# Five modulation parts summed by TensorE with the weights stationary, VectorE's other parts spread thinner over both v sweeps

## The chip, the cores and the metric

The kernel runs on one core of one Trainium2 chip. Five engines work in it, each through its own instruction stream: TensorE (PE; its weight loads are shown apart as PEld), VectorE (DVE), ScalarE (ACT), GpSimd (POOL) and SyncE (SP), which issues most of the transfers from HBM. TensorE's clock has two levels, 1.2 and 2.4 GHz; the profile shows the granted level as 0.50 and 1.00. The metric is the device time of one execution in microseconds.

## What is computed

A two-layer trunk over 128 context tokens and 256 latent tokens with 1024 channels. Layer 0 has windowed attention with pooling channels, layer 1 a convolution module; each is followed by PEER, a retrieval among 16,384 experts. Ahead of each of these four steps stands a normalisation that is modulated by a conditioning vector (`c_ctx` for the context tokens, `c` for the latent ones), and each step's result is gated by it:

```python
def adaln(cvec, w, b):
    m = jax.nn.silu(cvec) @ w + b
    return jnp.split(m[:, None, :], 6, axis=-1)

    mp = adaln(c_ctx[None, :], mod_w[l], mod_b[l])      # per layer l; ms likewise with c
    hp = modulate(rms_norm(xp, norm_mix_g[l]), mp[0], mp[1])     # h * (1 + scale) + shift
    ...                                                          # attention or convolution
    xp = xp + mp[2] * op
    hp = modulate(rms_norm(xp, norm_ffn_g[l]), mp[3], mp[4])
    xp = xp + mp[5] * peer(hp, ...)                     # xs likewise with ms

def conformer_conv(h, w1, b1, w_dw, b_dw, ln_g, ln_b, w2, b2):
    a = h @ w1 + b1
    a = a[..., :CONV_DIM] * jax.nn.sigmoid(a[..., CONV_DIM:])
    a = depthwise_conv(a, w_dw, width=31) + b_dw
    a = jax.nn.silu(layer_norm(a, ln_g, ln_b))
    return a @ w2 + b2
```

So there are twelve modulation parts, six per layer (shift, scale, gate, twice); each is the product of two vectors with a 1024x1024 matrix in fp32, and `mod_w` holds 48 MB in all.

## The kernel before

The activations are kept transposed, 128 channels on the partitions, eight chunks (`KC`) of channels, 384 tokens. Projections run through 512 KB weight blocks: SP loads a block into the ring `raw` (four slots, `load`, `stream`), ScalarE makes its rounded half `w_hi` (L691), GpSimd the rest `w_lo` (L599), and TensorE multiplies three times (L1511 to L1513, L1528 to L1530). A program of this kind has no scheduler: each engine runs the order in which the code is written, and semaphores tie the engines together.

In order of time there are: the head with the first norm; the projection `in` with ten blocks; attention (before it VectorE's rope, L1153 to L1155, then TensorE's scores, L1561; nine `in` blocks stand ahead of the first scores); `out`; the norm, the query projection and the choice of experts; the sweep over 128 u blocks; the **first v sweep** (L1745, 760.0 to 1304.4 us); the convolution with its norm, `w1` (16 blocks), the depthwise taps (TensorE at L1652 for some channel chunks, VectorE at L1247 for the others, spread over w1 and after it), mean and variance (L1663, L1667) and `w2` (eight blocks); and then queries, u sweep and **second v sweep** (2053.2 to 2516.2 us) of layer 1. In a v sweep SP loads the v blocks, VectorE weighs gathered rows and assembles the operand (L1432), ScalarE loads stored activations and applies the weights (L936 and on).

A modulation part is eight blocks of 512 KB, its matrix transposed: an output channel per partition. Part 0 (the first shift) is different before: TensorE keeps the two conditioning columns `cvec` stationary and passes its rows through in 512 columns (`first_shift`, L1772), ScalarE copies the two rows of sums, and TensorE turns them into columns (L1777). The other 88 blocks are summed by VectorE: `mod_group` (L1047) multiplies a block, 128x1024, by one of the two conditioning vectors that all partitions hold (`c_all`, in the tile `keys`, 1 MB, which ScalarE's `conditioning` passes through Silu), and sums along the row; two groups per block, and every four blocks `mod_bias` (L1053). The blocks come through a ring of four slots, `mod_w` in `hots` or later `mod_late` in `work`; SP loads a block when the group four blocks earlier is summed (`mod_load`). Eight blocks (part 1, the scale) are summed in the head, twelve in a loop ahead of the rope, twelve during attention and `out`, and 56 in the first v sweep, four per eight v blocks; for these SP loads c again at the start of that sweep, since the PEER keys have taken its place, and ScalarE waits for it there. The loads of `in` blocks 4 to 9 stand in SP's queue between pairs of modulation loads.

Of the kernel before, what the change touches and what calls it, by code (L numbers as in the profile page):

```python
# [38 lines left out]
P = 128  # L39
# [78 lines left out]
SUM_BLOCKS = MOD_BLOCKS - KC  # L118
MSLOTS = 4
MOD_EARLY = 4 * KC  # L120
MOD_FIRST = KC
LATE_MODS = MOD_EARLY - 12
MOD_ROUNDS = (SUM_BLOCKS - MOD_EARLY) // MSLOTS
# [61 lines left out]
def build(nc, io):  # L185
    ctx = ExitStack()
    with ctx:
# [71 lines left out]
        a_out = ga[:, :, :].rearrange("p a t -> p (a t)")[:, 0:4 * ND].rearrange("p (a t) -> p a t", a=4)  # L259
        unread = ga[:, :, :].rearrange("p a t -> p (a t)")[:, 0:D].bitcast(BF16).rearrange("p (g d) -> p g d", g=2)  # L260
# [42 lines left out]
        shift_rows = work[0:2, sums_at + 5 * D:sums_at + 6 * D]  # L303
        assert qk_at + 3 * D <= v_at and sums_at + 6 * D <= place[0]
# [5 lines left out]
        odd = region(2, CONV_OUT)  # L310
        tap_sum = (ps[:, 6, 0:CONV_OUT], ps[:, 7, 0:CONV_OUT])
# [36 lines left out]
        shift_summed = sem("shift_summed")  # L348
        shift_copied = sem("shift_copied")
        shift_done = sem("shift_done")  # L350
# [98 lines left out]
        def _(sp):  # L449
# [26 lines left out]

            def gates(i, span, n):
# [5 lines left out]
            def mod_load_late(k):  # L483

                sp.dma_start(mod_late[:, k, :], one(io["mod_w"], MOD_EARLY + k)).then_inc(mod_raw[k], 16)
# [15 lines left out]
            n = MOD_FIRST  # L501
# [5 lines left out]
            for m in range(RING):  # L507
                if n < MOD_EARLY - 8:
                    mod_load(n)
                    n += 1  # L510
                stream("out", m, 1, 1)
# [7 lines left out]
            for layer in range(DEPTH):  # L519
# [20 lines left out]
                if layer == 0:  # L540
                    sp.wait_ge(s_done, HS)
                    conditioning()
                    for k in range(MSLOTS):
                        mod_load_late(k)

                def turn(i, final, mods):

                    for j in range(TURN):
# [10 lines left out]
                        if j // 8 in mods and j % 2:  # L559
                            sp.wait_ge(mod_summed, i * TURN + (2 * MOD_EARLY - 8 + j + 1))  # L560
                            k = j % 8 // 2
                            sp.dma_start(mod_late[:, k, :],
                                         one(io["mod_w"], i * (TURN // 8 * MSLOTS) + (MOD_EARLY + j // 8 * MSLOTS + k))
                                         ).then_inc(mod_raw[k], 16)

                if layer == 0:

                    turn(0, False, range(1, 4))
                    with sp.Fori(1, TURNS - 1) as i:
                        turn(i, False, range(4))  # L570
                    turn(TURNS - 1, True, range(MOD_ROUNDS - 4 * (TURNS - 1)))
                else:
                    with sp.Fori(0, TURNS - 1) as i:
                        turn(i, False, ())
                    turn(TURNS - 1, True, ())
                if layer == 0:
                    sp.wait_ge(mod_summed, 2 * SUM_BLOCKS)
# [98 lines left out]
        def _(act):  # L676
# [31 lines left out]
            nc.scalar.activation(cvec[:, :, :], cvec[:, :, :], ACT.Silu).then_inc(c_ready, 1)  # L708
            conditioning(1)
# [36 lines left out]
            def gated(name, layer, part):  # L746

                m0 = M0[name]
                act.wait_ge(mod_ready, [MOD_EARLY - 2 * KC, SUM_BLOCKS][layer] // MSLOTS)
# [175 lines left out]
            def experts(layer):  # L925
# [48 lines left out]
                if layer == 0:  # L974
                    conditioning(2)
# [40 lines left out]
        def _(dve):  # L1016
# [23 lines left out]
            def mod_group(i, step, block, k, g, ring=mod_w):  # L1040
# [9 lines left out]
            def mod_bias(i, step, block):  # L1050
                dve.wait_ge(mod_summed, i * (2 * step) + (2 * (block + MSLOTS)))
                at = bass.ds(i * step + (block + KC), MSLOTS)
                tt(mod[:, at, :], sums[:, :, :], broad(mod_b[:, at], [P, MSLOTS, 2], 2), ALU.add).then_inc(mod_ready, 1)  # L1053

            def mod_four(i):
                for k in range(MSLOTS):
                    for g in range(2):
                        mod_group(i, MSLOTS, 0, k, g)
# [36 lines left out]
            def normalise(n):  # L1095
# [7 lines left out]
                if n == 0:  # L1103

                    dve.wait_ge(c_ready, 2)
                    rounds(dve, MOD_FIRST // MSLOTS, mod_four, peel=True)
                    dve.wait_ge(mod_ready, MOD_FIRST // MSLOTS)
                    mod_scales([0])
                    dve.wait_ge(shift_done, 1)
# [750 lines left out]
```

## Time and profile before

| | us |
|---|---|
| median of 3 runs | 2535.1 (2529.44 to 2536.3) |
| profiled execution | 2537.79 |
| its span | 2536.0 |
| head, up to the first product of `in` | 0 to 47.1 |
| `in`, and wait for the rope | 47.1 to 114.3 |
| attention, `out` | 114.3 to 235 |
| norm, queries, choice of experts | 235 to 404 |
| u sweep, layer 0 | 404 to 760.0 |
| first v sweep | 760.0 to 1304.4 |
| convolution, with its norm | 1304.4 to 1510 |
| norm, queries, choice of experts | 1510 to 1703 |
| u sweep, layer 1 | 1703 to 2053.2 |
| second v sweep | 2053.2 to 2516.2 |

TensorE is busy 91% of the span, VectorE 69%, GpSimd 44%, ScalarE 36%. In a row of the timeline the first number is the start, the second the time until the end of the last of the merged instructions, and brackets tell how long the engine had been idle and what released it. A row by stretch gives each engine's busy time, TensorE's granted clock, the share of the 16 DMA engines' time and what they moved.

### The profile page before, as it was taken

How to read it: one execution, taken by the hardware profiler on the slowest of the kernel's cores; microseconds unless marked ns; L12 is line 12 of the kernel's file. 1: busy time of each engine (PE TensorE's matmuls, PEld its weight loads, DVE VectorE, ACT ScalarE, POOL GpSimd, SP SyncE). 2: the span in 40 equal slices, each digit the busy share in tenths (PEclk: the TensorE clock that was granted, in tenths of full speed). 3: DMA queues.
4: the chain of work that ended last, by engine and by line, in shares of the span. 5: the costliest groups of instructions: out<-in, count | busy, mean ns of one | idle time of the engine just before them, and what ended most of it. 6: DMA issues, size and time to landing. Idle time of an engine off the chain costs nothing.

```text
span 2536.0 us, 38385 instructions
## 1 busy us (share of the span) xinstructions
PE 2296.9 (91%) x11829; PEld 1702.4 (67%) x11829; DVE 1752.9 (69%) x3945; ACT 911.0 (36%) x1694; POOL 1110.3 (44%) x612
## 2 busy tenths in 40 slices
PE   6797999999998888888989779999999989999998
PEld 3676999999983333333359469989999854444443
DVE  7986798878435766677768955898886345545555
ACT  3253445666541111111034354556666520000002
POOL 2613487777872222222215034677777841111110
PEclk8798999999999999899899889999999999999999
DMA  7423368999999999999954022588999999999995
GB/s 300 158 77 125 109 225 289 371 380 392 380 401 399 389 397 404 391 393 400 377 202 133 0 67 100 167 270 329 383 387 386 391 394 397 402 407 405 400 402 188
DMA packets 195783, 771.19 MB, mean 304 GB/s; under 512 B 21728, under 2 KB 22880, under 8 KB 160224
## 3 DMA queue, kind: packets, MB, share of 16 engines
q1 hardware_dynamic: 120512, 402.81, 42.8%
q0 software_dynamic: 36864, 268.45, 26.7%
q10 hardware_dynamic: 38304, 98.71, 10.0%
q8 instruction: 45, 0.74, 0.1%
q14 instruction: 58, 0.48, 0.1%
HBM read 701.08 MB, written 68.81 MB: 304 GB/s over the span
## 4 chain that ended last, share of the span: by engine, by line
PE 50%; DMA 18%; issue 13%; DVE 11%; POOL 6%; ACT 1%; ACTq 0%; SPq 0%; DVEq 0%; POOLq 0%
PE ps L1745 23%; DMA raw<-in_v 11%; PE ps L1511 7%; PE ps L1512 7%; PE ps L1513 7%; POOL w_lo L599 5%; DMA raw<-in_u 4%; PE ps L1727 4%; DVE ga L1047 1%; DVE ps L1328 1%; DVE work L1330 1%; DMA w_hi<-g_dram 1%; PE ps L1680 1%; ACT w_hi L691 1%; DVE work L1305 1%
## 5 line engine op out<-in xcount | busy, mean ns | idle before, releaser
L599 POOL TENSOR_TENSOR w_lo<-raw,w_hi 128x1024 fp32r<-128x1024 f32 x330 | 799.5, 2432 | 594.5 <-ACT w_hi L691 593.6
L1745 PE MATMUL ps<-raw,work 128*128 128x512 f32 x2048 | 913.4, 607 | 95.1 <-DMA raw<-in_v 82.5
L1745 PEld LDWEIGHTS ps<-raw,work 128*128 128x128 f32 x2048 | 393.9, 194 | 613.4 <-issue 572.7
L1511 PE MATMUL ps<-h_hi,w_hi 128*128 128x256 f32 (+1 forms) x2560 | 776.0, 303 | 26.3 <-POOL w_lo L599 26.2
L1512 PE MATMUL ps<-h_lo,w_hi 128*128 128x256 f32 (+1 forms) x2560 | 757.6, 296 | 0.0
L1513 PE MATMUL ps<-h_hi,w_lo 128*128 128x256 f32 (+1 forms) x2560 | 757.1, 296 | 0.0
L1511 PEld LDWEIGHTS ps<-h_hi,w_hi 128*128 128x128 f32 x2560 | 495.0, 193 | 35.0 <-POOL w_lo L599 32.6
L1512 PEld LDWEIGHTS ps<-h_lo,w_hi 128*128 128x128 f32 x2560 | 495.4, 194 | 0.0
L1513 PEld LDWEIGHTS ps<-h_hi,w_lo 128*128 128x128 f32 x2560 | 494.6, 193 | 0.0
L691 ACT ACTIVATE w_hi<-raw 128x1024 fp32r<-128x1024 f32 x330 | 347.6, 1056 | 130.0 <-DMA raw<-in_u 54.1
L936 ACT ACTIVATE wgt<-dots (+1 forms) x256 | 53.1, 208 | 755.3 <-DVE uv_stat L1389 218.3
L617 POOL DMA_INDIRECT work<-in_uv,picked x64 | 73.1, 1142 | 245.9 <-DVE ps L1381 236.8
L617 POOL DMA_INDIRECT hots<-in_uv,picked x64 | 73.8, 1153 | 242.2 <-DVE ps L1381 231.1
L1432 DVE TENSOR_TENSOR work<-work,w_hi 128x256 f32<-128x256 f32 x128 | 53.8, 424 | 175.4 <-PE ps L1745 130.1
L1408 DVE TENSOR_SCALAR hots<-ps,work 128x128 f32<-128x128 f32 x512 | 173.6, 400 | 0.0
L956 ACT ACTIVATE work<-ps 128x512 f32<-128x512 f32 x128 | 145.5, 1137 | 66.0 <-PE ps L1727 62.2
L1432 DVE TENSOR_TENSOR work<-work 128x256 f32<-128x256 f32 x128 | 53.6, 423 | 161.8 <-PE ps L1745 120.3
L919 ACT ACTIVATE ga<-ps 128x256 f32<-128x256 f32 x256 | 97.6, 381 | 176.9 <-PE ps L1513 172.4
L1047 DVE CUSTOM_DVE_ANT_0 ga<-work,keys 128x1024 bf16<-128x1024 f32 x112 | 136.3, 1217 | 20.7 <-issue 11.0
L1404 DVE TENSOR_TENSOR hots<-ps,work 128x512 f32<-128x512 f32 x128 | 87.8, 686 | 82.3 <-PE ps L1727 82.2
L617 POOL DMA_INDIRECT hf<-in_uv,picked x64 | 71.7, 1121 | 155.2 <-DVE ps L1381 151.4
L1727 PE MATMUL ps<-hots 128*128 128x128 f32 x1024 | 135.3, 275 | 1.6 <-ACT work L956 1.6
(196 smaller groups left out, 2416.2 us busy)
## 6 DMA issues: line engine op xcount, KB each, us to landing
raw<-in_u SPq DMA_DIRECT2D x256, 512.0 KB, 6.1
raw<-in_v SPq DMA_DIRECT2D x256, 512.0 KB, 8.8
a_dram<-ga ACTq DMA_DIRECT2D x128, 256.0 KB
g_dram<-work ACTq DMA_DIRECT2D x16, 2048.0 KB, 12.3
work<-a_dram ACTq DMA_DIRECT2D x120, 256.0 KB, 8.0
work<-in_mod_w SPq DMA_DIRECT2D x56, 512.0 KB, 13.0
hots<-in_mod_w SPq DMA_DIRECT2D x32, 512.0 KB, 3.6
raw<-in_wq SPq DMA_DIRECT2D x32, 512.0 KB, 3.5
```

The lines of the kernel that those rows point to most:

```text
L599: nc.gpsimd.tensor_tensor(w_lo[:, m % RING, :], raw[:, m % RING, :], w_hi[:, m % RING, :].bitcast(F32), ALU.subtract).then_inc(lo_ready, 1)
L617: nc.gpsimd.indirect_dma_start(out=uv_rows[q % UVBUFS], out_offset=None, in_=io[f"uv{layer}"], in_offset=bass.IndirectOffsetOnAxis(ap=pick ...
L691: nc.scalar.activation(w_hi[:, m % RING, :], raw[:, m % RING, :], ACT.Copy).then_inc(hi_ready, 1)
L956: nc.scalar.activation(stage[:, s, :, tok:tok + TOK].rearrange("p k t -> p t k"), ps[:, ACC, :].rearrange("p (t k) -> p t k", k=N_KEYS), A ...
L1047: nc.vector.tensor_tensor_reduce(unread[:, g, :], ring[:, k, :], c_all[:, g, :], 1.0, 0.0, ALU.mult, ALU.add, accum_out=sums[:, k, g:g + 1 ...
L1408: last = ts(oh1[:, b, q, :], iota_p, col_key[:, 0, tok], col_g[:, tok], ALU.is_equal, ALU.mult)
L1432: tt(wf[:, j % WBUFS, :].rearrange("p (c t) -> p c t", t=CHUNK), a_in[:, j % (2 * A_PAIRS), :].rearrange("p (c t) -> p c t", t=CHUNK), g_i ...
L1511: mm(out, w_hi[:, s, cols], h_hi[:, k, first:], start=n == 0, stop=False)
L1512: mm(out, w_hi[:, s, cols], h_lo[:, k, first:], start=False, stop=False)
L1513: last = mm(out, w_lo[:, s, cols], h_hi[:, k, first:], start=False, stop=n == KC - 1)
L1727: last = mm(ps[:, ACC, q * P:(q + 1) * P], oh2[:, b, q, :], oh1[:, b, q, :], start=True, stop=True)
L1745: last = mm(ps[:, Y_DENSE[NT - ND_TILES + t] + half, :], wf[:, b, t * P:(t + 1) * P], raw[:, s, half * 512:(half + 1) * 512], start=first, ...
```

## The change

Parts 0, 1, 8, 9 and 10 (layer 0's first shift and scale; layer 1's gate of the convolution and its second shift and scale) are now made by TensorE with the weights stationary: a chunk of 512 KB, 128 input channels by 1024 output channels, is eight stationary 128x128 tiles, and the two conditioning columns of `cvec` are passed through each (`part_sums`). The result lies with the channels on the partitions, in PSUM, and needs no turning. 16 chunks stand in the head behind the first column sums (`first_parts`), 24 in the convolution: five ahead of w1, one after each of w1's blocks 6 to 12, six between the taps on TensorE and the mean, six ahead of w2. They come through their own ring of five slots, `part_w`, loaded by SP between the blocks of w1 and w2.

VectorE sums the seven other parts, 56 blocks: twelve in the loop, now its first and with the group for the context vector reading c from PSUM (`c_ps`, written by ScalarE), twelve in attention and `out` as before, 24 in the first v sweep (one per four v blocks), eight in the second. c is loaded a third time, at the second sweep's start. In the head SP issues c's load behind the 16 chunks.

```diff
+PE_PARTS = (0, 1, 8, 9, 10)
+SUM_PARTS = (2, 3, 4, 5, 6, 7, 11)
+PSLOTS = 5
+CHUNKS_NORM, CHUNKS_W1, CHUNKS_MEAN, CHUNKS_W2 = range(0, 5), range(5, 12), range(12, 18), range(18, 24)
-MOD_EARLY = 4 * KC
-MOD_FIRST = KC
+MOD_EARLY = 3 * KC
+MOD_FROM = (MOD_EARLY, 6 * KC)
+MOD_ROUNDS = (3 * KC // MSLOTS, KC // MSLOTS)
...
+        c_ps = ps[:, 6:8, :].rearrange("p a b -> p (a b)")
...
+            for n in range(KC):
+                if n % 4 == 3:
+                    load("in", n // 4, n // 4)
+                head_chunk(n)
+            for n in range(KC, HEAD_CHUNKS):
+                head_chunk(n)
             conditioning()
-            for k in range(KC):
-                if k % 4 == 3:
-                    load("in", k // 4, k // 4)
-                sp.dma_start(shift_w[k], one(io["shift_w"], k)).then_inc(shift_loaded[k], 16)
-                mod_load(k)
+            for n in range(MSLOTS):
+                mod_load(n)
...
-            n = MOD_FIRST
+            n = MSLOTS
             for m in range(RING, 10):
                 for _ in range(2):
                     mod_load(n)
                     n += 1
                 stream("in", m, 1, 1)
...
-                if layer == 0:
-                    sp.wait_ge(s_done, HS)
-                    conditioning()
-                    for k in range(MSLOTS):
-                        mod_load_late(k)
+                sp.wait_ge(s_done, (layer + 1) * HS)
+                conditioning()
+                for k in range(MSLOTS):
+                    mod_load_late(layer, k)
...
-                        if j // 8 in mods and j % 2:
+                        if span in mods and j % 4 == 3:
...
-                    stream("w1", RING, 16 - RING, 4)
-                    stream("w2", 0, 8, 4)
+                    sp.wait_ge(rows_used, SLOTS)
+                    for n in CHUNKS_NORM:
+                        part_chunk(n)
+                    stream("w1", RING, 2, 2)
+                    for n in range(5, 10):
+                        part_chunk(n)
+                        stream("w1", n + 1, 1, 1)
+                    ...
...
             nc.scalar.activation(cvec[:, :, :], cvec[:, :, :], ACT.Silu).then_inc(c_ready, 1)
+            act.wait_ge(c_loaded, 16)
+            nc.scalar.activation(c_ps, c_all[:, 0, :], ACT.Silu).then_inc(c_ready, 1)
+            act.wait_ge(c_ready, 2)
             conditioning(1)
...
-                    act.wait_ge(shift_summed, 1)
-                    nc.scalar.activation(shift_rows, ps[0:2, ACC + 2:ACC + 4, :].rearrange("p a b -> p (a b)"),
-                                         ACT.Copy).then_inc(shift_copied, 1)
...
-                if layer == 0:
-                    conditioning(2)
+                conditioning(2 + layer)
...
-                nc.vector.tensor_tensor_reduce(unread[:, g, :], ring[:, k, :], c_all[:, g, :], 1.0, 0.0,
+                nc.vector.tensor_tensor_reduce(unread[:, g, :], ring[:, k, :],
+                                               c_all[:, g, :] if g or first is None else first, 1.0, 0.0,
                                                ALU.mult, ALU.add, accum_out=sums[:, k, g:g + 1]).then_inc(mod_summed, 1)
...
-                    dve.wait_ge(c_ready, 2)
-                    rounds(dve, MOD_FIRST // MSLOTS, mod_four, peel=True)
-                    dve.wait_ge(mod_ready, MOD_FIRST // MSLOTS)
+                    dve.wait_ge(part_done, HEAD_CHUNKS)
+                    settle(tt(mod[:, 0:2 * KC, :], ps[:, ACC + 1, 0:4 * KC].rearrange("p (a b) -> p a b", b=2),
+                              broad(mod_b[:, 0:2 * KC], [P, 2 * KC, 2], 2), ALU.add))
                     mod_scales([0])
...
             def convolution():
-                blocks("w1")
+                part_chunks(CHUNKS_NORM)
+                blocks("w1", beside=CHUNKS_W1)
...
+                pe.wait_ge(conv_taken, KC - CONV_DVE)
+                part_chunks(CHUNKS_MEAN)
...
+                part_chunks(CHUNKS_W2)
                 blocks("w2")
...
-            def first_shift():
...
+            def part_sums(w, bank, col, k):
+
+                for o in range(KC):
+                    last = mm(ps[:, bank, col + 2 * o:col + 2 * o + 2], w[:, o * P:(o + 1) * P], cvec[:, k, :],
+                              start=k == 0 and o == 0, stop=k == KC - 1 and o == KC - 1)
+                last.then_inc(part_done, 1)
```

The change moves instructions in three places that matter below. First, SP's queue in the head. `in_c` is c, `in_shift_w` part 0, `in_mod_w` VectorE's blocks and `in_part_w` TensorE's chunks. Before (the last two rows then go on in turn, eight of each):

```order
L489 DMA ident<-in_c_ident 128x128
L489 DMA cvec<-in_c_cols 128x16
L452 DMA keys<-in_c 128x2048
L494 DMA work<-in_shift_w 128x1024
L457 DMA hots<-in_mod_w 128x1024
```

After:

```order
L505 DMA cvec<-in_c_cols 128x16
L486 DMA work<-in_part_w 128x1024 x3
L467 DMA raw<-in_in 128x1024
L486 DMA work<-in_part_w 128x1024 x4
L467 DMA raw<-in_in 128x1024
L486 DMA work<-in_part_w 128x1024 x9
L458 DMA keys<-in_c 128x2048
L463 DMA hots<-in_mod_w 128x1024 x4
L467 DMA raw<-in_in 128x1024 x2
```

c stood ahead of everything but the small tables, and stands behind 16 chunks and two `in` blocks now; only four of VectorE's blocks are loaded ahead of its loop, where eight were.

Second, SP's queue in the first v sweep, between its first v blocks, before:

```order
L461 DMA raw<-in_v 128x1024 x2
L562 DMA work<-in_mod_w 128x1024
L461 DMA raw<-in_v 128x1024
L480 DMA w_hi<-g_dram 128x2x512
L461 DMA raw<-in_v 128x1024
L562 DMA work<-in_mod_w 128x1024
L461 DMA raw<-in_v 128x1024 x2
```

The same part of the sweep after:

```order
L467 DMA raw<-in_v 128x1024 x7
L496 DMA work<-g_dram 128x2x512
L467 DMA raw<-in_v 128x1024 x2
L576 DMA work<-in_mod_w 128x1024
L467 DMA raw<-in_v 128x1024
L496 DMA work<-g_dram 128x2x512
L467 DMA raw<-in_v 128x1024 x3
L496 DMA work<-g_dram 128x2x512
L576 DMA work<-in_mod_w 128x1024
```

Between two modulation loads there were two v blocks, and there are four.

Third, TensorE at the end of the convolution, from w1's last products over the taps, mean and variance to w2. Before:

```order
L1513 MATMUL ps<-h_hi,w_lo 128x384
L1544 REGISTER_ALU
L1544 COMPARE_AND_BRANCH
L1652 MATMUL ps<-work,hots 128x399 x62
L1663 MATMUL ps<-work,ones 128x399 x8
L1667 MATMUL ps<-work,ones 128x399 x8
L1528 MATMUL ps<-h_hi,w_hi 128x384
```

After:

```order
L1551 MATMUL ps<-h_hi,w_lo 128x384
L1699 MATMUL ps<-work,hots 128x399 x62
L1817 MATMUL ps<-cvec,work 128x2 x48
L1710 MATMUL ps<-work,ones 128x399 x8
L1714 MATMUL ps<-work,ones 128x399 x8
L1817 MATMUL ps<-cvec,work 128x2 x48
L1566 MATMUL ps<-h_hi,w_hi 128x384
```

Two groups of 48 products with two columns each, six chunks, stand ahead of the mean's and of w2's products; the wait for the taps' results on VectorE now comes behind the first of them.

## Rows read from the trace of the kernel before

**Rows 1.** By stretch: first v sweep, second v sweep (first line: the columns)

```profile
core 0: us, PE busy (x) PEld busy (x) DVE busy (x) ACT busy (x) POOL busy (x), PEclk, DMA share, GB/s
760.00:1304.40 544.40, 467.73 (x1025) 200.43 (x1026) 369.02 (x610) 63.82 (x181) 118.80 (x77) 0.94 0.98 386
2053.20:2516.20 463.00, 445.60 (x1026) 193.91 (x1027) 241.34 (x368) 41.35 (x165) 73.43 (x77) 1.00 0.98 385
```

**Rows 2.** TensorE's waits for v blocks, first and second sweep (us, times, longest)

```profile
PE ps L1745 <- DMA raw<-in_v: 67.1, 23, 8.1
...
PE ps L1745 <- DMA raw<-in_v: 15.4, 11, 3.6
```

**Rows 3.** DMA issues: the first sweep's modulation blocks (count, KB, us to landing)

```profile
work<-in_mod_w SPq DMA_DIRECT2D x56, 512.0 KB, 13.0
```

**Rows 4.** Timeline (start, us): TensorE, then ScalarE, early in the first sweep

```profile
779.51 20.85 PE L1745 MATMUL ps<-raw,work 128*128 128x512 f32 x43 [9.02 <-DVE work L1432]
...
773.87 1.91 ACT L703 ACTIVATE keys<-keys 128x2048 f32<-128x2048 f32 x1 [11.77 <-DMA keys<-in_c]
```

**Rows 5.** Weight loads (ns min/median/max), ranges and clock by stretch, passes at 37.76

```profile
40.70:42.70 2.00, 1.94 (x16) 1.86 (x16) 2.00 (x5) 0.00 (x0) 0.00 (x0) 1.00 1.14 356
43.20:47.10 3.90, 0.00 (x0) 0.00 (x0) 3.30 (x12) 1.49 (x4) 0.00 (x0) 0.50 1.03 393
...
1703.20:1704.90 1.70, 1.64 (x8) 1.64 (x9) 0.06 (x2) 0.31 (x1) 1.31 (x1) 0.50 1.01 424
...
L1777 PEld LDWEIGHTS ps<-ident,work x16: 181/187/187, 40.7 to 42.4; 2*128 2x128 f32 x16
...
L1772 PEld LDWEIGHTS ps<-work,cvec x32: 80/85/127, 16.0 to 38.6; 128*2 128x2 f32 x32
...
L1716 PEld LDWEIGHTS ps<-ident,work x12: 179/230/231, 406.6 to 1704.2; 128*128 128x128 f32 x12
...
1703.26 1.14 PEld L1716 LDWEIGHTS ps<-ident,work 128*128 128x128 f32 x6 [4.45 <-DVE gate_s L1371]
...
37.76 1.88 PE L1772 MATMUL ps<-work,cvec 128*2 128x512 f32 x4 [1.93 <-DMA work<-in_shift_w]
```

**Rows 6.** Timeline: column sums, first products, first scores (TensorE); first scaling (VectorE)

```profile
8.91 7.15 PE L1551 MATMUL ps<-hf,ones 128*128 128x384 f32 x16 [8.91 <-DVE hf L1139]
...
47.14 0.66 PE L1528 MATMUL ps<-h_hi,w_hi 128*128 128x384 f32 x1 [4.46 <-DVE h_lo L1127]
...
114.26 0.79 PE L1561 MATMUL ps<-work 64*128 64x128 f32 x2 [15.15 <-DVE work L1155]
...
44.63 1.41 DVE L1118 SCALAR_TENSOR_TENSOR hf<-x,scales,uv_stat 128x128 f32<-128x128 f32 x4 [0.32 <-DVE mod L1110]
```

**Rows 7.** Loop before attention, in block 8, taps (timeline; L1247 by line)

```profile
55.77 1.22 DVE L1047 CUSTOM_DVE_ANT_0 ga<-hots,keys 128x1024 bf16<-128x1024 f32 x1
...
56.91 3.37 DVE L1047 CUSTOM_DVE_ANT_0 ga<-hots,keys 128x1024 bf16<-128x1024 f32 x1
...
109.14 1.48 DVE L1153 TENSOR_TENSOR work<-ps,work 128x1280 f32<-128x1280 f32 x1
...
83.53 0.43 SPq L461 DMA_DIRECT2D raw<-in_in  x1
...
L1247 DVE SCALAR_TENSOR_TENSOR ps<-work,dw,ps x168: 626/631/635, 1334.1 to 1448.6; 128x399 f32<-128x399 f32 x168
```

**Rows 8.** Convolution: w1 by stretch, then timeline of TensorE and VectorE

```profile
1320.70:1390.50 69.80, 69.54 (x384) 69.27 (x385) 60.75 (x126) 28.12 (x45) 37.80 (x16) 0.96 0.36 113
...
1320.72 0.66 PE L1528 MATMUL ps<-h_hi,w_hi 128*128 128x384 f32 x1 [8.33 <-DVE h_lo L1127]
...
1449.90 1.70 PE L1663 MATMUL ps<-work,ones 128*128 128x399 f32 x2 [12.64 <-DVE work L1251]
...
1468.25 0.66 PE L1528 MATMUL ps<-h_hi,w_hi 128*128 128x384 f32 x1 [7.78 <-DVE h_lo L1136]
...
1349.22 0.74 DVE L1226 SCALAR_TENSOR_TENSOR work<-ps,b,work 128x128 f32<-128x128 f32 x2 [1.08 <-PE ps L1513]
```

More of the change, by code:

```diff
@@ L302, in build @@
                    for n in range(count)]
-        shift_rows = work[0:2, sums_at + 5 * D:sums_at + 6 * D]
-        assert qk_at + 3 * D <= v_at and sums_at + 6 * D <= place[0]
+        assert qk_at + 3 * D <= v_at and sums_at + 5 * D <= place[0]
         a_pad = region(KC, CONV_IN, at=0)
@@ L347, in build @@
         shift_loaded = [sem(f"shift_loaded{k}") for k in range(KC)]
-        shift_summed = sem("shift_summed")
-        shift_copied = sem("shift_copied")
-        shift_done = sem("shift_done")
+        part_loaded = [sem(f"part_loaded{k}") for k in range(PSLOTS)]
+        part_done = sem("part_done")
+        parts_taken = sem("parts_taken")
         mod_summed = sem("mod_summed")
@@ L506, in _ @@
                 stream("in", m, 1, 1)
[L507 to L511, printed above, removed]
+            stream("out", 0, RING, RING)
             while n < MOD_EARLY - 4:
@@ L576, in _ @@
[L576 to L580 removed]
+                assert MOD_ROUNDS == (2 * (TURNS - 1), 2)
+                turn(0, False, (1,))
+                with sp.Fori(1, TURNS - 1) as i:
+                    turn(i, False, () if layer else (0, 1))
+                turn(TURNS - 1, True, ())
@@ new lines, in _ @@
+                if layer == 0:
+                    sp.wait_ge(mod_summed, 2 * MOD_FROM[1])
+                    sp.dma_start(keys[:, :, :], io["keys"][1]).then_inc(keys_loaded, 16)
+                    sp.wait_ge(rows_used, SLOTS)
[5 more added lines that the diff above has]
+                        stream("w1", n + 1, 1, 1)
+                    for n in range(10, 15):
+                        stream("w1", n + 1, 1, 1)
+                        part_chunk(n)
+                    for n in range(15, 17):
+                        part_chunk(n)
+                    stream("w2", 0, RING, RING)
+                    for n in range(17, 22):
+                        part_chunk(n)
+                    stream("w2", RING, 2, 2)
+                    for n in range(22, 24):
+                        part_chunk(n)
+                    stream("w2", RING + 2, 2, 2)
@@ L1036, in _, with mod_group @@
             dve.wait_ge(first_loaded, 5 * 16)
-            def mod_group(i, step, block, k, g, ring=mod_w):
+            def mod_group(i, step, block, k, g, ring=mod_w, first=None):
                 if k == 0 and g == 0:
@@ L1057, in mod_four @@
                     for g in range(2):
-                        mod_group(i, MSLOTS, 0, k, g)
+                        mod_group(i, MSLOTS, 0, k, g, first=c_ps)
                 mod_bias(i, MSLOTS, 0)
@@ L1259, in convolution @@
                 taps(len(pending))
+                dve.wait_ge(part_done, HEAD_CHUNKS + KC)
+                at = slice((6 + 2) * KC, (6 + 3) * KC)
+                settle(tt(mod[:, at, :], ps[:, ACC + 1, 0:2 * KC].rearrange("p (a b) -> p a b", b=2),
+                          broad(mod_b[:, at], [P, KC, 2], 2), ALU.add))
+                tt(gb2[:, :, :], mod[:, at, :], broad(cvecs[:, 3, :], [P, KC, 2], 2), ALU.mult).then_inc(parts_taken, 1)
                 dve.wait_ge(mean_done, 1)
@@ L1271, in convolution @@
                 pipelined(scaled, low_operand)
+                dve.wait_ge(part_done, HEAD_CHUNKS + 3 * KC)
+                for at, src in ((6 + 3, ps[:, ACC, CONV_OUT + 1:CONV_OUT + 1 + 2 * KC]), (6 + 4, ps[:, ACC + 2, 0:2 * KC])):
+                    cols = slice(at * KC, (at + 1) * KC)
+                    last = tt(mod[:, cols, :], src.rearrange("p (a b) -> p a b", b=2), broad(mod_b[:, cols], [P, KC, 2], 2),
+                              ALU.add)
+                    last.then_inc(parts_taken, 1)
+                dve.wait_ge(parts_taken, 3)
+                mod_scales([3])
                 for k in range(KC):
@@ L1532, in project_pair, with blocks @@
                             last.then_inc(block_done, 1)
-            def blocks(name, chunks=()):
+            def blocks(name, chunks=(), beside=()):
                 m, r = M0[name], R0[name]
@@ L1543, in blocks @@
                     project(0, 4, m + j, r + j)
+                if beside:
+                    for j in range(4, dict(SEGMENTS)[name]):
+                        project(0, 4, m + j, r + j)
+                        if j - 6 in range(len(beside)):
+                            part_chunks(beside[j - 6:j - 5])
+                    return
                 with pe.Fori(1, dict(SEGMENTS)[name] // 4) as i:
```

113 lines of the change are left out of this document (55 added, 58 removed).

## The prediction

> **What bounds the kernel now.** I read the busy time by stretch first. The two sweeps over the 128 v blocks do the same work twice, but the first lasts 544.4 us and the second 463.0, both with the DMA engines 98% busy at 386 and 385 GB/s [rows 1]. TensorE's waits say the same: on v blocks 67.1 us in the first sweep, 15.4 in the second [rows 2]. What the first has and the second has not is 56 modulation blocks of 512 KB [rows 3] and the 1 MB of c: 58 units of 512 KB for 81.4 us, 1.40 us each; by bandwidth a unit is 524,288 B / 386 GB/s = 1.36 us. So the first sweep is bound by bytes. Elsewhere other things end last: in the head VectorE's sums of eight modulation blocks, behind which the first projection starts at 47.14; before attention VectorE's loop over twelve more blocks, behind which TensorE waits 15.15 us [rows 6, 7]; in the convolution first TensorE's w1, then VectorE's chain of taps, for whose end TensorE waits until 1449.90 [rows 8].
>
> The sum is made against the profiled execution, 2537.8 us (span 2536.0), 2.7 above the median 2535.1.
>
> **1. First sweep.** 32 of its 56 modulation blocks go: 32 x 1.36 = 43.5 us less (by 1.40 it would be 44.8). The floor does not get in the way: TensorE is busy 467.7 us there and VectorE 369.0 [rows 1], and VectorE loses 64 sums. I take **-43.5** (-40 to -45). The stop at its start stays: TensorE idles 9.02 us because ScalarE sat 11.77 us waiting for c [rows 4].
>
> **2. Second sweep.** It gains 8 blocks and c, 10 units, at 98% DMA: **+13.6**. ScalarE now waits for c here too, with everything it would store, load and weight behind it. In the first sweep that stop didn't stop the transfers, so it is within the unit price; the upper bound adds its 9.0 us: +22. Below, +10: TensorE's other waits could absorb some.
>
> **3. Price of a chunk.** A part is now eight chunks of eight fp32 products 128x128 by 128x2, each in two passes, so a chunk is 16 pairs of weight load and 2-column matmul. The nearest rows are the 16 pairs of the transposes at L1777, at full clock: their weight loads lie within 1.86 us, the last takes 0.187, so they start (1.86 - 0.187) / 15 = 0.112 us apart [rows 5]. A chunk is then 16 x 0.112 = **1.79 us**. The clock will not stay up: it stood at 0.50 (1.2 GHz) shortly after those pairs [rows 5]. A load of 128 columns took 187 ns at 2.4 GHz and 230 at 1.2 (L1716, where the clock was 0.50), one of 2 columns 85 and at its slowest 127 [rows 5]: the difference, the columns' part, is 102 and 103 ns at either clock, and the 43 ns that are added are overhead that pairs overlap. So I keep 1.79. The upper bound by rows is the pairs of L1716 with their slow loads, (1.14 - 0.23) / 5 = 0.18 us apart, but with 128 moving columns behind each [rows 5]: 2.9 us a chunk. Below, a pair cannot be cheaper than the columns' 102 ns: 1.63.
>
> Here two rules of one page can be weighed. The Trainium skill ("TensorE: Matmul & The Clock Gate", "LDWEIGHTS (loading the stationary operand)") prices a load by its columns alone, columns / 1.2 ns, 107 ns here, an estimate of 1.71 us a chunk; the 112 ns agree. Its "Part 1: The HAM clock gate (the "warmup" mystery)" has the gate pass only half the pulses to the array, and were the loads to go by that clock, this change would lose, as in rival A; the equal 102 and 103 ns speak against it.
>
> **4. Head.** Removed: 16 of VectorE's sums, the 512-column passes, ScalarE's copy and the transposes. Added on TensorE behind the column sums, which end at 16.06 [rows 6]: 16 chunks x 1.79 = 28.6, ending at 44.7, where VectorE's scaling began at 44.63 before [rows 6]: 0. Chunks arrive faster than they are used (17 units of 1.36 us are 23 us, and they start before the column sums end). But c now comes behind 16 chunks, and ScalarE's wait for it stands ahead of its root and first two w_hi. GpSimd's two passes for w_lo then fall beside VectorE's scaling, where each can cost a VectorE operation with two SBUF inputs about 2.15 us (3.37 - 1.22, [rows 7]): +4.5 (3 to 6).
>
> **5. Loop and attention.** The 24 sums of the loop run from 55.77 to 109.14, 53.4 us for 24 x 1.22 = 29.3 of work; the rest is collisions with GpSimd and three short biases [rows 7]. After the change every other sum reads c from PSUM. An operation with one PSUM input never lost anything: 626 to 635 ns over 168 taps, beside GpSimd's passes [rows 7]. Halving the 24 us of loss makes the loop some 12 us shorter; since a GpSimd pass that spares one sum often meets the next, I take -9. Against that, the loads of `in` move back in SP's queue: block 8, the last that stands before the first scores, was issued at 83.53 once six of the loop's twelve blocks were summed, and 15.6 us later, at 114.26 - 15.15 = 99.11, TensorE was through with it [rows 6, 7]; now it waits for ten of twelve. The loop starts at 60.3 and takes 53.4 - 9 = 44.4; the rope behind it, 5.1 us from VectorE's start at 109.14 to the first scores at 114.26 [rows 6, 7], ends at 109.8. Ten of twelve blocks are done at 60.3 + 37 = 97.3, and 97.3 + 15.6 = 112.9: block 8 comes last now. So 1.4 us are won; the 15.6 hold a block at low clock, which a busier TensorE may run faster, and I take **-2** for head and attention together (-9 if block 8 is quick and the loop loses less, +6 if the loop loses as often as before).
>
> **6. Convolution.** Ahead of w1 TensorE idles 8.33 us for the norm [rows 8]; five chunks take 8.95: +0.6. In w1, seven chunks after blocks 6 to 12. TensorE bounds this stretch (69.5 of 69.8 us) and VectorE's serial taps wait for it, 1.08 us per pair of blocks [rows 8], so 7 x 1.79 = 12.5 delay both: +12.5. Should the clock fall in each of these gaps, part of the next block (69.5 / 16 = 4.35 us) runs at half speed, some 2 us each time: +14 more. Against it, after a wait of 1.93 us the four passes at 37.76 still took 1.88 us, full speed [rows 5]; I take 0. Before the mean, six chunks (10.7) in the 12.64 us in which TensorE waits for the last taps: 0. That cover is thin; gone, it costs up to 10.7. Ahead of w2, six chunks (10.7) where it idled 7.78: +2.9. Sum **+16** (11 if VectorE catches up in w1, 30 if the clock falls in each gap). Chunks' loads are hidden: DMA is 36% busy there [rows 8]. The few VectorE operations on 16 columns that turn sums into mod, gb2 and scales lie in waits for TensorE: 0; without that cover, under 1 us.
>
> **Sum:** -43.5 + 13.6 - 2 + 16 = -15.9. From 2537.8 that is 2521.9, and against the median 2535.1 - 15.9 = **2519**. The terms' bounds, not all at once, give 2506 to 2538.
>
> **The rivals.**
> A, slower: weight loads go by the lower clock. A pair then takes 2 x 0.112 us and a chunk 3.6. The head's chunks end at about 68 (the first three at full clock: 16.06 + 3 x 1.79 + 13 x 3.6), +23, of which the shorter loop takes back 6.5 (the 4.5 of the head and the 2 above); the convolution pays 5 x 3.6 - 8.3 = 9.7, 12.5 in w1 (full clock there), 21.6 - 12.6 = 9, and 21.6 - 7.8 = 13.8, together 45. Sum: -29.9 + 16.5 + 45 = +31.6: 2567. Between 1.79 us (-15.9) and 3.6 (+31.6) the sign turns at a chunk of 2.4 us, 150 ns a pair. For it: the clock does fall. Against: the 102 and 103 ns.
> B: the wait for c at the second sweep's start idles TensorE on top of the bytes: +9, 2528. For it: TensorE is busy 445.6 of 463 us there, with little room to recover. Against: DMA stayed at 98%.
> C, the change doesn't bring its bytes' worth: part of the 81.4 us is the stop at the start and the clock (0.94 against 1.00), not bytes, and the first sweep gives only half, 22. Then -22 + 13.6 - 2 + 16 = +5.6: 2541. Against: the waits for v, 52 us apart.
>
> **How the numbers follow.** Forecast 0.66, A 0.12, B 0.12, C 0.10. A measurement of this kernel can tell about 0.3%, 7.6 us: faster is below 2527.5, slower above 2542.7. Of the forecast 0.57 is faster and 0.09 the same; of B 0.06 and 0.06; of C 0.02 faster, 0.06 the same, 0.02 slower; A is slower. Faster 0.65, same 0.21, slower 0.14. The range leaves out most of A and a little below: 2500 to 2547.
>
> **What would show it.** First sweep about 501 us, its waits for v near 25; second about 477. Pairs of the chunks 0.11 us apart, also at clock 0.50; first projection at about 51, first scores near 112. The last tap some 13 us later relative to w1's start, no wait of VectorE's for the mean's chunks, and w2's start 16 us later relative to the norm. It is wrong if a chunk takes over 2.4 us, if the first sweep stays above 515, or if the second passes 490.

## The result, and the profile after

The changed kernel is slower: 2544.42 us (median of 20 runs, 2538.89 to 2550.64) against 2529.11 (20 runs), a ratio of 1.0059, 95% interval 1.0049 to 1.0068, some 15 us. 2519 was forecast, 16 us faster than the median known then. The time lies in the stated range, but on the other side, on rival A's. The profiled executions are 2544.5 and 2537.8 us; the latter is 8.7 above its kernel's own median, which matters for the first sweep (see e5_cps).

The stages, from TensorE's first and last products in each (us):

| stage | before | after | change | forecast |
|---|---|---|---|---|
| start to the first product of `in` | 47.1 | 70.9 | +23.7 | +4.5 |
| to the first scores | 67.1 | 52.1 | -15.0 | -6.5 |
| attention to the end of the u sweep | 645.7 | 646.7 | +1.0 | 0 |
| first v sweep | 544.6 | 496.3 | -48.3 | -43.5 |
| norm ahead of w1, chunks | 16.2 | 20.8 | +4.6 | +0.6 |
| w1, chunks | 69.8 | 81.9 | +12.1 | +12.5 |
| taps and mean, chunks | 69.9 | 74.4 | +4.5 | 0 |
| to w2, chunks | 7.8 | 15.1 | +7.3 | +2.9 |
| w2 to the end of the u sweep | 585.0 | 584.2 | -0.8 | 0 |
| second v sweep | 462.9 | 480.4 | +17.5 | +13.6 |

Both sweeps did what was forecast. Busy time by stretch, columns as in [rows 1], first sweep, second sweep and w1:

```profile
769.73:1265.84 496.11, 460.40 (x1024) 196.46 (x1025) 298.67 (x472) 63.82 (x181) 95.57 (x77) 0.97 0.99 390
2042.50:2522.70 480.20, 450.83 (x1024) 195.01 (x1025) 259.60 (x402) 63.80 (x181) 80.61 (x77) 0.98 0.97 382
1286.83:1368.70 81.87, 81.63 (x497) 81.34 (x498) 56.19 (x112) 25.71 (x39) 37.83 (x16) 0.97 0.46 161
```

TensorE's waits for v blocks, first and second sweep, which answer to [rows 2]:

```profile
PE ps L1793 <- DMA raw<-in_v: 26.0, 20, 5.7
...
PE ps L1793 <- DMA raw<-in_v: 19.5, 13, 6.0
```

The DMA engines are as busy as before, and the waits went from 67.1 to 26.0 us in the first sweep.

The loss is in the chunks. TensorE's timeline in the head, then the clock in two stretches of it and over all chunks, and its weight loads by line (L1817 is `part_sums`):

```profile
17.30 50.52 PE L1817 MATMUL ps<-cvec,work 128*128 128x2 f32 x256
70.88 0.66 PE L1566 MATMUL ps<-h_hi,w_hi 128*128 128x384 f32 x1 [3.06 <-DVE h_lo L1153]
...
19.30:21.30 2.00, 2.00 (x20) 2.00 (x19) 0.00 (x0) 0.00 (x0) 0.00 (x0) 1.00 0.57 162
25.30:35.30 10.00, 10.00 (x49) 10.00 (x48) 0.00 (x0) 0.00 (x0) 0.00 (x0) 0.50 0.50 158
17.30:67.82 50.52, 50.52 (x257) 50.43 (x255) 4.28 (x4) 8.54 (x9) 5.00 (x2) 0.54 0.62 226
...
L1817 PEld LDWEIGHTS ps<-cvec,work x640: 186/333/338, 17.0 to 1458.0; 128*128 128x128 f32 x160
```

The 16 chunks were to take 28.6 us and take 50.5. At clock 1.00, 20 pairs (a weight load and its 2-column product) go through in 2.0 us; at 0.50, 49 in 10.0, 0.205 us a pair and 3.3 us a chunk. By the records TensorE never stops in these 50 us (its weight loads fill 50.43 of 50.52), and the clock falls all the same. The convolution shows the same (TensorE's timeline: ahead of w1, one chunk between w1's blocks, ahead of the mean, mean, ahead of w2):

```profile
1273.71 13.26 PE L1817 MATMUL ps<-cvec,work 128*128 128x2 f32 x80
...
1318.74 1.84 PE L1817 MATMUL ps<-cvec,work 128*128 128x2 f32 x16
...
1411.15 17.69 PE L1817 MATMUL ps<-cvec,work 128*128 128x2 f32 x96 [0.68 <-ACT work L894]
1428.70 6.99 PE L1710 MATMUL ps<-work,ones 128*128 128x399 f32 x16
...
1443.01 15.42 PE L1817 MATMUL ps<-cvec,work 128*128 128x2 f32 x96
1458.30 0.67 PE L1566 MATMUL ps<-h_hi,w_hi 128*128 128x384 f32 x1
```

A chunk alone between two blocks of w1 takes 1.84 us, as forecast; five in a row take 13.26 instead of 8.95, six take 17.69 and 15.42 instead of 10.7. The mean's wait for VectorE [rows 8] is gone: the mean's 16 products now start right behind the chunks.

The loop ahead of attention was better than forecast (VectorE's first two sums, and the rope behind the last), and c came later (ScalarE's first Silu):

```profile
79.51 1.21 DVE L1075 CUSTOM_DVE_ANT_0 ga<-hots,ps 128x1024 bf16<-128x1024 f32 x1
...
80.65 2.67 DVE L1075 CUSTOM_DVE_ANT_0 ga<-hots,keys 128x1024 bf16<-128x1024 f32 x1
...
116.12 1.49 DVE L1179 TENSOR_TENSOR work<-ps,work 128x1280 f32<-128x1280 f32 x1
...
46.66 1.03 ACT L736 ACTIVATE ps<-keys 128x1024 f32<-128x1024 f32 x1 [34.96 <-DMA keys<-in_c]
```

The loop takes 36.6 us where it took 53.4 [rows 7]; the sums with c in PSUM all take 1.21 to 1.22.

### The profile page after: what moved, and what is told of

It is laid out like the page before. It is cut to its first block, busy times and chain, and to the rows that moved or that the text cites. A ratio compares the mean times of both kernels' runs of the same rounds, so it can differ in the third digit from the quotient of the medians.

```text
span 2542.7 us, 38958 instructions
## 1 busy us (share of the span) xinstructions
PE 2375.3 (93%) x12421; PEld 1793.9 (71%) x12421; DVE 1670.6 (66%) x3812; ACT 933.1 (37%) x1711; POOL 1087.3 (43%) x612
## 4 chain that ended last, share of the span: by engine, by line
PE 54%; DMA 15%; issue 13%; DVE 10%; POOL 5%; ACT 1%; SPq 0%; ACTq 0%; DVEq 0%; POOLq 0%
PE ps L1793 24%; DMA raw<-in_v 10%; PE ps L1549 7%; PE ps L1550 7%; PE ps L1551 7%; POOL w_lo L625 5%; PE ps L1775 4%; DMA raw<-in_u 4%; PE ps L1817 2%; DVE ps L1367 1%; DVE work L1369 1%; PE ps L1728 1%; DMA a_dram<-ga 1%; DVE ga L1075 1%; ACT w_hi L717 1%
## 5 line engine op out<-in xcount | busy, mean ns | idle before, releaser
L643 POOL DMA_INDIRECT uv_stat<-in_uv,picked x64 | 66.6, 1041 | 152.8 <-DVE ps L1420 149.2
```

What stands on the lines that cost most here:

```text
L643: nc.gpsimd.indirect_dma_start(out=uv_rows[q % UVBUFS], out_offset=None, in_=io[f"uv{layer}"], in_offset=bass.IndirectOffsetOnAxis(ap=pick ...
```

## The experiments

The theory after this reading: it is the granted clock that doubles the weight loads, and the clock falls because the products pass only two columns each. The rivals: many loads in a row are slow for another reason, and the clock only goes along with it; the sweeps lose by their stops; the chunks in w1 or the head's loss are made up elsewhere. "Kernel before" in the ratios is run beside each on the same chip.

**e1_hold: a wide product ahead of each chunk of the head.**

```diff
                     pe.wait_ge(shift_loaded[n % KC], 16 * (n // KC + 1))
+                    mm(ps[:, PROJ, :], ones[:, :], shift_w[n % KC][:, 0:512], start=True, stop=True)
                     part_sums(shift_w[n % KC], ACC + 1, n // KC * 2 * KC, n % KC)
```

> The changed kernel, with one fp32 product of 512 moving columns (two passes, 0.86 us at full clock, into an unused PSUM bank) put ahead of each of the head's 16 chunks; nothing else differs. Theory (clock): a chunk's 16 pairs of weight load and 2-column product take 1.72 us at 2.4 GHz and 3.3 us at 1.2, and it is the granted clock that doubles them; the wide products keep the clock at 1.00, a chunk with its product takes 2.6 us, the 16 end at about 59 to 60 instead of 67.8, and the kernel is some 8 us faster than the changed one (2536). Rival (series): many small loads in a row are slow whatever the clock, about 3.2 us a chunk; then the 16 take 16 x 4.1 = 65 us, end at about 83, and the kernel is some 15 us slower than the changed one.

2575.79 us, 1.0200 (1.0174 to 1.0226) of before, 31 more than the changed kernel: both expectations missed. TensorE's timeline, the second chunk, and the fourth with its wide product:

```profile
19.62 1.84 PE L1817 MATMUL ps<-cvec,work 128*128 128x2 f32 x16
21.32 1.10 PE L1826 MATMUL ps<-work,ones 128*128 128x512 f32 x2
...
24.61 2.06 PE L1826 MATMUL ps<-work,ones 128*128 128x512 f32 x2
26.46 3.41 PE L1817 MATMUL ps<-cvec,work 128*128 128x2 f32 x16
```

One wide product per chunk did not hold the clock; it fell to 0.50 in the third chunk and stayed there, and from then on every round took 5.12 us. But the two prices stand side by side: a chunk 1.84 and 3.41, the wide product 1.10 and 2.06. Products of 512 columns, which have nothing to do with a row of loads, change by the same factor at the same moment. That speaks for the clock and against the rival, without having held it.

**e2_now1: no chunks inside w1.**

```diff
-PE_PARTS = (0, 1, 8, 9, 10)
-SUM_PARTS = (2, 3, 4, 5, 6, 7, 11)
-CHUNKS_NORM, CHUNKS_W1, CHUNKS_MEAN, CHUNKS_W2 = range(0, 5), range(5, 12), range(12, 18), range(18, 24)
+PE_PARTS = (0, 1, 9, 10)
+SUM_PARTS = (2, 3, 4, 5, 6, 7, 8, 11)
+CHUNKS_NORM, CHUNKS_MEAN, CHUNKS_W2 = range(0, 5), range(5, 11), range(11, 16)
...
-                blocks("w1", beside=CHUNKS_W1)
+                blocks("w1")
```

> The changed kernel without the chunks between w1's blocks: part 8 goes back to VectorE, whose eight blocks are summed in the first v sweep (32 blocks there instead of 24, four in every second group of eight v blocks); the 16 chunks left in the convolution stand 5 ahead of w1, 6 ahead of the mean, 5 ahead of w2. Theory: the chunks in w1 run at full clock but lie wholly on the path (w1 81.9 us with them, 69.8 without): -12; one chunk less ahead of w2 -2; eight blocks more in the first sweep at 1.36 us each +10.9; together about -3. Rival: VectorE's taps set w1's length, and the chunks there cost nothing: then +8 to +9.

2536.79 us, 1.0030 (1.0013 to 1.0047), some 7 less than the changed kernel. Its first sweep and w1 by stretch:

```profile
766.46:1272.10 505.64, 459.91 (x1027) 196.44 (x1028) 314.99 (x506) 63.84 (x182) 101.31 (x77) 0.97 0.99 391
1293.00:1362.30 69.30, 69.06 (x386) 68.77 (x386) 55.95 (x111) 25.60 (x40) 37.96 (x16) 0.97 0.40 137
```

w1 is 12.6 us shorter, the first sweep 9.5 longer. So the chunks in w1 lie wholly on the path, at 1.8 us each, and a block in the sweep costs less than that, 9.5 / 8 = 1.2 us. The rival falls. The sweep varies from trace to trace: with 32 blocks it took 501.8 to 509.9 us in four traces (e2_now1, e6_wide, e8_c_sooner, e9_head_ve), with 24 blocks 496.3 to 496.9 in three (changed kernel, e1_hold, e4_oldhead). The means, 506.2 and 496.7, give the same 1.2. So even at full clock these seven chunks were a loss, some 3 us, but a small one beside that variation.

**e3_early_c: c loaded during the u sweeps.**

```diff
-                stream(f"u{layer}", 0, N_KEYS - SPAN, 4)
+                stream(f"u{layer}", 0, SPAN, 4)
+                sp.wait_ge(s_done, (layer + 1) * HS)
+                conditioning()
+                stream(f"u{layer}", SPAN, N_KEYS - 2 * SPAN, 4)
...
-                sp.wait_ge(s_done, (layer + 1) * HS)
-                conditioning()
                 for k in range(MSLOTS):
                     mod_load_late(layer, k)
```

> The changed kernel with c's 1 MB loaded for both v sweeps while the 16th u block is loaded, some 300 us earlier, instead of at the v sweep's start; ScalarE's Silu stays where it is. Theory (stop): TensorE's stops of 7.1 and 7.5 us at the two sweeps' starts, which wait for ScalarE's wait for c, are lost time: they shrink to under 2 us and the kernel gains 8 to 12 us. Rival (bytes): the transfers go on during the stop, so the sweeps end when their bytes are through; they only lose c's 2.7 us each, which the u sweeps (DMA 97% busy) pay: 0 to -3.

2543.77 us, 1.0063 (1.0042 to 1.0084): no difference from the changed kernel. TensorE early in the first and in the second sweep:

```profile
793.84 6.56 PE L1794 MATMUL ps<-raw,work 128*128 128x512 f32 x9 [15.22 <-DMA raw<-in_v]
...
2066.30 9.06 PE L1794 MATMUL ps<-raw,work 128*128 128x512 f32 x14 [14.56 <-DMA raw<-in_v]
```

The same in the changed kernel:

```profile
787.39 18.14 PE L1793 MATMUL ps<-raw,work 128*128 128x512 f32 x35 [7.12 <-DVE work L1471]
...
2060.49 19.89 PE L1793 MATMUL ps<-raw,work 128*128 128x512 f32 x39 [7.45 <-DVE work L1471]
```

The stops for c (9.0 us in [rows 4], 7.1 and 7.5 in the changed kernel) are gone, and TensorE waits for v blocks a little later, 15.2 and 14.6 us at once. The sweeps take 494.5 and 478.1 us where they took 496.3 and 480.4: they end when their bytes are through. The prediction's rival B falls with this.

**e4_oldhead: the head of the kernel before, the rest as changed.** Parts 0 and 1, c first in the queue and the loop without c in PSUM, word for word as before.

> The changed kernel with the head and the loop ahead of attention of the kernel before (part 0 by 512-column passes, part 1 summed by VectorE, c loaded first and read from SBUF alone); convolution and both v sweeps as changed. Theory: the head's chunks at 1.2 GHz cost 23.7 us, of which the loop with c in PSUM gave back 14; undone, the first v sweep starts 9 to 10 us earlier and the kernel is that much faster than the changed one: about 2535. Rival: the lost time of the head is made up later (the stages behind it are bound by transfers that could run ahead); then no difference.

2528.80 us, 0.9992 (0.9973 to 1.0011), 15.6 less than the changed kernel, where 9 to 10 were expected, and level with the kernel before. The first product stands at 47.71 and the first scores at 114.32, 8.7 sooner than changed; the first sweep starts 13.2 sooner, 4.5 of it between attention and the sweep, where nothing differs and the traces of these kernels lie between 642 and 649 us. The head's loss is not made up. With the head out, the rest is level: the sweeps' gain, some 24 us, goes into the convolution's 28.

**e5_cps: the kernel before, with c in PSUM for the early sums.**

```diff
+            act.wait_ge(c_loaded, 16)
+            nc.scalar.activation(c_ps, c_all[:, 0, :], ACT.Silu).then_inc(c_ready, 1)
+            act.wait_ge(c_ready, 2)
             conditioning(1)
...
-                        mod_group(i, MSLOTS, 0, k, g)
+                        mod_group(i, MSLOTS, 0, k, g, first=c_ps)
```

> The kernel before with one thing of the change: in the head and in the loop ahead of attention, VectorE's sums for the context vector read c from PSUM, where ScalarE writes a second Silu of it. Theory: the loop, 53.4 us before and 36.6 in the changed kernel, becomes some 15 us shorter, and the first scores, which waited for it, start at about 103 instead of 114: 9 to 11 less than before (2520). Rival: the in blocks, whose loads stand between the modulation loads, set the first scores by then: 3 less at most.

2524.14 us, 0.9962 (0.9945 to 0.9979): 8 less than the kernel before beside it (2532.01), where 9 to 11 were expected. The first scores, and the first sweep by stretch:

```profile
103.89 0.79 PE L1566 MATMUL ps<-work 64*128 64x128 f32 x2 [13.99 <-DVE work L1160]
...
749.45:1286.80 537.35, 469.95 (x1027) 201.11 (x1028) 369.48 (x610) 63.84 (x182) 119.25 (x77) 0.95 0.99 391
```

The scores start 10.4 us sooner and still wait for VectorE, so the rival falls. The sweep does the work of [rows 1] in 537.3 us instead of 544.4, so some 7 us of the 544.4 seem to belong to that execution, which was 8.7 above its median. Against 537.3, the change's first sweep gains 41, and the sum of the table's changes (+6.7) becomes some +14, near the 15 of the medians.

**e6_wide: the same chunks with 64 columns.** As e2_now1, with the two conditioning columns passed 32 times over:

```diff
+                columns = cvec[:, k, :].unsqueeze(1).broadcast_to([P, WIDE // 2, 2])
                 for o in range(KC):
-                    last = mm(ps[:, bank, col + 2 * o:col + 2 * o + 2], w[:, o * P:(o + 1) * P], cvec[:, k, :],
+                    last = mm(ps[:, bank, col + WIDE * o:col + WIDE * (o + 1)], w[:, o * P:(o + 1) * P], columns,
                               start=k == 0 and o == 0, stop=k == KC - 1 and o == KC - 1)
```

> As e2_now1, but each of the chunks' products passes 64 columns instead of two: the two conditioning columns 32 times over, so that a part fills one PSUM bank and VectorE reads two columns of each 64. Theory (clock, and what it follows): the product's 64 columns hide behind the weight load at full clock, and TensorE now has enough to do for the clock to stay at 1.00; a chunk takes about 1.75 us everywhere, the head's first product starts at about 48 instead of 70, the first scores at about 102, the mean's chunks go into the wait for the taps, and the convolution is some 14 us shorter: 2503, 34 less than e2_now1. Rival (loads): the clock looks at nothing that the width changes, it falls as before and a chunk stays at 3.3 us: 2537. One product of 512 columns per chunk did not hold it in e1_hold, which speaks for the rival.

2504.65 us, 0.9887 (0.9852 to 0.9921): 32 less than e2_now1, and faster than both kernels. TensorE in the head, its clock there, its weight loads, and the chunks ahead of w1, of the mean and of w2:

```profile
16.91 28.69 PE L1816 MATMUL ps<-cvec,work 128*128 128x64 f32 x256
54.89 0.66 PE L1564 MATMUL ps<-h_hi,w_hi 128*128 128x384 f32 x1 [9.28 <-DVE h_lo L1151]
...
27.00:37.00 10.00, 10.00 (x92) 10.00 (x91) 0.00 (x0) 0.00 (x0) 0.00 (x0) 1.00 0.85 294
...
L1816 PEld LDWEIGHTS ps<-cvec,work x512: 186/192/192, 16.6 to 1426.7; 128*128 128x128 f32 x171
...
1272.14 9.04 PE L1816 MATMUL ps<-cvec,work 128*128 128x64 f32 x80
...
1392.82 10.93 PE L1816 MATMUL ps<-cvec,work 128*128 128x64 f32 x96 [0.68 <-ACT work L887]
1403.58 4.92 PE L1708 MATMUL ps<-work,ones 128*128 128x399 f32 x14
1409.75 0.94 PE L1708 MATMUL ps<-work,ones 128*128 128x399 f32 x2 [1.25 <-DVE work L1275]
...
1418.01 9.04 PE L1816 MATMUL ps<-cvec,work 128*128 128x64 f32 x80
```

With nothing but more columns (and a PSUM bank for each part) the clock stays at 1.00 and all 512 loads take 186 to 192 ns; 256 pairs take 28.69 us, 0.112 each, the price of the prediction. The 32 us are found where the chunks stand: the first scores come at 109.0 instead of 122.7, and the convolution is 162.4 us with its 16 chunks (180.5 in e2_now1, 163.7 before without any). The mean waits for VectorE's taps again, so the six chunks ahead of it are free. The rival falls: it was the clock, and it stayed up with the wider products. No run tried a width between two and 64 columns, and the changed kernel itself, with its chunks in w1, was not run wide. What is left in the head is 9.28 us of waiting, where 3.1 are usual: c comes late, and with it VectorE's preparation falls beside GpSimd's first two passes:

```profile
47.33 4.98 POOL L618 TENSOR_TENSOR w_lo<-raw,w_hi 128x1024 fp32r<-128x1024 f32 x2 [46.13 <-ACT w_hi L710]
...
47.53 2.59 DVE L1110 SCALAR_TENSOR_TENSOR uv_stat<-uv_stat 128x384 f32<-128x384 f32 x1
...
50.44 1.90 DVE L1090 SCALAR_TENSOR_TENSOR scales<-mod,gains 128x16 f32<-128x16 f32 x1
```

In the trace of before, VectorE's same two operations took 0.56 and 0.18 us.

**e7_v0all: part 11 in the first sweep too.**

```diff
-MOD_FROM = (MOD_EARLY, 7 * KC)
-MOD_ROUNDS = (4 * KC // MSLOTS, KC // MSLOTS)
+MOD_FROM = (MOD_EARLY, 8 * KC)
+MOD_ROUNDS = (5 * KC // MSLOTS, 0)
```

> As e6_wide, with part 11's eight blocks in the first v sweep too (40 there, three groups of four per 32 v blocks), so that the second sweep has neither modulation blocks nor c. Theory: the second sweep gets its 17.5 us back (480 to 463), the first pays 8 x 1.36 = 10.9: 6 to 7 less than e6_wide. Rival (bytes alone): only c's 1 MB goes, 2.7 less.

2506.09 us, 0.9901 (0.9865 to 0.9937): the same as e6_wide, neither expectation being told apart from nothing. The second sweep got 11.8 us back (474.7 to 462.9), the first paid 5.3 (509.9 to 515.2), and the rest varied by as much. Where the blocks are put between the two sweeps makes no difference that was measured.

**e8_c_sooner: c behind the eighth chunk of the head.**

```diff
+            conditioning()
             for n in range(KC, HEAD_CHUNKS):
                 head_chunk(n)
-            conditioning()
```

> As e6_wide, with c's load moved in SP's queue from behind the 16th chunk of the head to behind the eighth. Theory: in e6_wide the chunks are done at 45.6 us, but the first product starts only at 54.9, because c lands late and ScalarE's two Silus stand ahead of its root; with c sooner the first product starts at about 48 and the first scores about 6 us sooner: 2498 to 2500. Rival: c's 1 MB now delays chunks 8 to 15, TensorE waits for them, and nothing is won.

2497.36 us, 0.9880 (0.9858 to 0.9901). TensorE:

```profile
16.37 28.69 PE L1816 MATMUL ps<-cvec,work 128*128 128x64 f32 x256
48.19 0.66 PE L1564 MATMUL ps<-h_hi,w_hi 128*128 128x384 f32 x1 [3.12 <-DVE h_lo L1151]
```

The chunks take as long as before, and the first product comes 6.7 us sooner, the first scores at 101.1 instead of 109.0. By the ratios to the kernel before, e8_c_sooner and e6_wide overlap; the place in the trace is what shows the gain.

**e9_head_ve: VectorE's head, with c in PSUM, and e6_wide's convolution and sweeps.** The head of the kernel before as in e4_oldhead, with c_ps as in e5_cps.

> As e6_wide, with the head of the kernel before (part 0 by 512-column passes, part 1 by VectorE) and c_ps in it and in the loop as in e5_cps; convolution and sweeps as in e6_wide. Theory: at full clock it is all the same who makes part 1, since both heads end when their 8 MB are through and worked off; first scores at 104 as in e5_cps, 5 us sooner than e6_wide, all of it owed to c being first in the queue, and so the same as e8_c_sooner within 3 us: 2499. Rival: with VectorE free of the 16 sums the head by TensorE is better, and e9_head_ve is 5 or more slower than e8_c_sooner.

2497.24 us, 0.9869 (0.9845 to 0.9893), the same as e8_c_sooner; first scores at 106.2. At full clock it makes no measurable difference who makes part 1, so the head's part of the change is not worth anything that was measured. What is: c in PSUM (8 us, e5_cps), and the 16 wide chunks in the convolution together with the lighter first sweep, which bring the rest.

## Why the prediction was wrong

**Step 3, the price of a chunk, failed**, and with it the sign. 1.79 us holds at clock 1.00 (1.84 between w1's blocks; 28.69 / 16 = 1.79 in e6_wide). At 0.50 it is 3.3. The prediction's own sign of being wrong, a chunk of over 2.4 us, was there. The clock's fall was foreseen, its price was not: the equal column parts of 102 and 103 ns hang on L1716's 230 ns at the lower clock, and these loads are not like the others. The trace of before had the right row right behind the one I read, weight loads of the kernel's own projections at the same lower clock (timeline of TensorE's loads):

```profile
1704.39 0.34 PEld L1511 LDWEIGHTS ps<-h_hi,w_hi 128*128 128x128 f32 x1
```

340 ns against 187. With this row the prediction's own subtraction gives 340 - 127 = 213 ns for the columns, an estimate; 205 from pair to pair were measured. Why L1716's loads took 230 there stays open. The Trainium skill's rule ("TensorE: Matmul & The Clock Gate", "LDWEIGHTS (loading the stationary operand)"), 107 ns for 128 columns, agrees with 112 at 2.4 GHz and is out by nearly two at 1.2 (205); its "Part 1: The HAM clock gate (the "warmup" mystery)", by which the array gets only half the pulses in its cold state, is the rule that these rows bear out, 205 against 112, though here the clock fell without an idle gap.

**Step 4, head:** +4.5 forecast, +23.7 measured; 50.5 - 28.6 = 21.9 of it is the clock. The collisions that made up the +4.5 cost nothing in the changed kernel: the chunks ran until 67.8, and VectorE waited 10.7 us for them. At full clock (e6_wide) the head is +7.7: ScalarE's two Silus and root end only at 46.3, because c lands late, and the two collisions then do come, 3.8 us of the 7.7. With c sooner (e8_c_sooner) it is +1.

**Step 5, loop:** the mechanism was right and its size too small: -16.8 instead of -9 (53.4 to 36.6). Before, nine of the 24 sums took some 2.15 us longer than their 1.22; now six do, all with c in SBUF, by 1.0 to 1.5 us. That is 12.4 us, about the halving (12) from which the step started before it took 9. Another 4.2 are the three short additions of the bias, which the step did not count as a gain: two of them were held up before, none is now (the third one, before and after):

```profile
106.71 2.51 DVE L1053 TENSOR_TENSOR mod<-sums,mod_b 128x8 f32 x1 [0.26 <-DVE sums L1047]
...
115.86 0.17 DVE L1082 TENSOR_TENSOR mod<-sums,mod_b 128x8 f32 x1 [0.27 <-DVE sums L1075]
```

Block 8 came last before the scores, as forecast, and 15.0 of the 16.8 us reached them; the head's +23.7 outweighed that.

**Step 6, convolution:** +28.5 instead of +16. w1's +12.5 was right (12.1, and all of it on the path, e2_now1). The other three terms were mis-sized by the chunk's price, +16.4 instead of +3.5. At full clock they come to about nothing (e6_wide). The clock didn't fall in w1's gaps, as assumed.

**Steps 1 and 2, sweeps:** right. Forecast -43.5, measured -48 in these two executions and -41 against the sweep of e5_cps; forecast +13.6, measured +17.5 (and +13.7 against the second sweep of e5_cps, 466.7). With that, rival C falls too. That the stop for c costs nothing beyond its bytes was right (e3_early_c).

**Rival A** named the mechanism and the side. Its head was right, +23 against +23.7. Its +31.6 us was twice what came: in the convolution (45 against 28.5) it let the clock be low in whole groups, while the first 30 to 50 pairs behind dense work still ran at 1.00, and it took 3.6 us for a chunk; and it gave the loop 6.5 where 15.0 came. That the time still lies in the stated range is luck: the range left out most of A, and the time came back into it because A was out in the convolution and the loop.

## What to carry to other kernels

Matrix-vector work with the weights stationary is priced at the clock that it leaves behind: a long row of loads with two columns each ran at the lower clock here, and repeating the same two columns 32 times cost nothing and brought a pair from 0.205 to 0.112 us. Read the price of an operation at the lower clock from several lines of the trace before trusting one. Where VectorE sums beside a busy GpSimd, put one operand into PSUM: that alone gave 8 us; and bytes moved out of a stretch that DMA bounds pay only if the place that takes them has engine time to spare (seven chunks in w1 cost 12.6 us, where the eight blocks of their part had cost the sweep 9.5).

## What the runs showed of the hardware that was not expected

- TensorE's clock fell to 0.50 under work that kept the engine busy without a gap (50.52 us for 256 pairs in the changed kernel, their weight loads 50.43 of it); with 64 columns instead of two, the same loads ran at 1.00 throughout (28.69 us). One product of 512 columns (two passes) per 16 pairs did not hold it (e1_hold), one w1 block per 16 pairs did (1.84 us a chunk).
- The weight loads of 128 columns follow the clock: 186 to 192 ns at 1.00, 333 to 338 at 0.50; pairs 0.112 and 0.205 us apart.
- Taking a stop of TensorE of 7.1 and 7.5 us out of two sweeps whose DMA is 97 to 99% busy gave nothing (e3_early_c); a wait for v blocks of 15 us stood in each of them instead.
